# Feed-forward in column pairs: seven block products in place of eight on half of the k-tiles, weight block sums on VectorE

## The reference

```python
x = x + jnp.concatenate([ret, att], axis=-1) @ w_out[layer]
h = rms_norm(x, norm2_g[layer])
x = x + jnp.square(jax.nn.relu(h @ w_ff1[layer])) @ w_ff2[layer]
```

## Time and profile before

| | us |
|---|---|
| median of 3 runs | 1158.16 (1158.1 to 1158.98) |
| span of the profiled execution | 1156.3 |
| TensorE busy | 1149.4 (99%) |
| VectorE busy | 650.8 (56%) |
| ScalarE busy | 530.9 (46%) |

### The profile page before, as it was taken

One profiled execution on the slowest core, in us unless ns is written; L12 is line 12 of the kernel. 1 busy time (PEld: TensorE's weight loads), 2 busy tenths in 40 slices (PEclk: granted clock), 3 DMA queues, 4 the chain that ended last, 5 costly groups with the idle time before them and its releaser, 6 DMA issues.

```text
span 1156.3 us, 14920 instructions
## 1 busy us (share of the span) xinstructions
PE 1149.4 (99%) x5426; PEld 977.8 (85%) x5426; DVE 650.8 (56%) x845; ACT 530.9 (46%) x730; POOL 23.5 (2%) x26
## 2 busy tenths in 40 slices
PE   9999999999999999999999999999999999999998
PEld 8889889889888888888888888888888888888887
DVE  6667667667667555545545555554555555555543
ACT  6545445445444554444433445343444433444342
POOL 0000000000000000000000000000000000000000
PEclk9999999999999999999999999999999999999999
DMA  9745445445454545545555543555445555454552
GB/s 355 310 172 192 162 161 193 159 175 176 177 193 177 188 173 194 185 178 194 207 182 193 194 188 150 218 186 207 187 181 181 185 200 195 158 209 179 198 195 77
DMA packets 34918, 219.23 MB, mean 190 GB/s; under 512 B 3920, under 2 KB 4432, under 8 KB 12112
## 3 DMA queue, kind: packets, MB, share of 16 engines
q1 hardware_dynamic: 34896, 218.93, 52.3%
HBM read 216.81 MB, written 2.10 MB: 189 GB/s over the span
## 4 chain that ended last, share of the span: by engine, by line
PE 97%; DMA 2%; DVE 1%; SPq 0%; ACT 0%; issue 0%; ACTq 0%
PE acc L333 31%; PE acc L335 31%; PE acc L334 31%; DMA raw<-in_w_ret 1%; PE bankB L361 1%; PE bankA L361 1%; DMA raw<-in_w_att 1%; PE bankC L377 0%; PE bankC L388 0%; PE bankD L403 0%; PE bankD L383 0%; DVE w_lo L692 0%; PE bankA L395 0%; PE bankC L411 0%; PE bankC L412 0%
## 5 line engine op out<-in xcount | busy, mean ns | idle before, releaser
L692 DVE TENSOR_TENSOR w_lo<-raw,w_hi 128x1024 fp32r<-128x1024 f32 (+1 forms) x416 | 488.2, 1181 | 352.7 <-ACT w_hi L503 350.3
L503 ACT ACTIVATE w_hi<-raw 128x1024 fp32r<-128x1024 f32 (+1 forms) x416 | 420.9, 1025 | 354.2 <-PE acc L335 345.8
L333 PE MATMUL acc<-w_hi,hT_hi 128*128 128x512 f32 (+1 forms) x1024 | 392.1, 383 | 1.8 <-DVE w_lo L692 1.8
L335 PE MATMUL acc<-w_hi,hT_lo 128*128 128x512 f32 (+1 forms) x1024 | 385.1, 376 | 0.0
L334 PE MATMUL acc<-w_lo,hT_hi 128*128 128x512 f32 (+1 forms) x1024 | 384.7, 376 | 0.0
L333 PE MATMUL acc<-w_hi,zT_hi 128*128 128x512 f32 x640 | 250.2, 391 | 0.0
L335 PE MATMUL acc<-w_hi,zT_lo 128*128 128x512 f32 x640 | 249.2, 389 | 0.0
L334 PE MATMUL acc<-w_lo,zT_hi 128*128 128x512 f32 x640 | 249.0, 389 | 0.0
L333 PEld LDWEIGHTS acc<-w_hi,hT_hi 128*128 128x128 f32 x1024 | 192.4, 188 | 31.9 <-DVE w_lo L692 3.0
L335 PEld LDWEIGHTS acc<-w_hi,hT_lo 128*128 128x128 f32 x1024 | 192.2, 188 | 30.4
L334 PEld LDWEIGHTS acc<-w_lo,hT_hi 128*128 128x128 f32 x1024 | 192.5, 188 | 29.1
(11 more groups left out here) (109 smaller groups left out, 365.6 us busy)
## 6 DMA issues: line engine op xcount, KB each, us to landing
raw<-in_w_up SPq DMA_DIRECT2D x64, 1024.0 KB, 4.8
raw<-in_w_down SPq DMA_DIRECT2D x64, 1024.0 KB, 4.8
raw<-in_w_ret SPq DMA_DIRECT2D x32, 1024.0 KB, 4.8
raw<-in_w_att SPq DMA_DIRECT2D x28, 768.0 KB, 4.3
raw<-in_w_out SPq DMA_DIRECT2D x16, 1024.0 KB, 4.9
raw<-in_w_att SPq DMA_DIRECT2D x8, 384.0 KB, 7.0
xs<-in_x SPq DMA_DIRECT2D x4, 512.0 KB, 13.6
out<-xs SPq DMA_DIRECT2D x8, 256.0 KB, 4.3
```

The costliest lines, as they stand in the source:

```text
L333: nc.tensor.matmul(o, hi[:, k, tile_cols(m)], wh, start=first, stop=False)
L335: mm = nc.tensor.matmul(o, lo[:, k, tile_cols(m)], wh, start=False, stop=last)
L503: nc.scalar.activation(w_hi[:, q % SLOTS, 0:PIECE_KT * n], raw[:, q // 2, (q % 2) * PIECE_KT * n:(q % 2 + 1) * PIECE_KT * n], ACT.Copy).th ...
L692: nc.vector.tensor_tensor(w_lo[:, q % SLOTS, 0:PIECE_KT * n], raw[:, q // 2, (q % 2) * PIECE_KT * n:(q % 2 + 1) * PIECE_KT * n], w_hi[:, q ...
```

## The change

**Column pairs.** The feed-forward works in 16 pairs p of two column groups: of every four, two are up and two down. Of a pair's 16 k-tiles, the first 8 are a 2 x 2 block problem: two blocks of 4 k-tiles by two row tiles on the left, and two by two column groups on the right, where a block of the weights is one slab. These eight block products are made as seven of a Winograd scheme (`product`, 12 matmuls each): Q1, P5, P6, Q2, P7, P3, P4. The other 8 k-tiles are four slabs as before, R1 to R4 (`rest`, 24 matmuls each). R1 and R2 go to the first column group and R3 and R4 to the second.

**Steps of a body.** PE's body p makes the rest of pair p-1 between the products of pair p, in the order R1, Q1, R2, P5, R3, P6, R4, Q2, P7, P3, P4. The code is unrolled. `w_hi` and `w_lo` are rings of 3 slabs, and a conversion is one instruction of 128 x 2048 (`hi_slab`, `lo_slab`); `hi_slab(s)` waits until slab s-3 is used. `raw` has 5 slots.

**Sums of weights.** P5, P6, P7 and P4 need a sum of slabs in `raw`, made in place by VectorE (`sum_slabs`), ahead of the conversion.

**Sums of products.** Q1, P6 and P7 share a bank, so ScalarE copies Q1 to `q1` (`keep_q1`) before P6, and VectorE makes u1, u3, u2 and v4 (128 x 512 each) out of banks and these. Four outputs follow for a pair: for up pairs `up_sum` makes `hid`, and ScalarE has relu and square; for down pairs `add_products` and `add_bank` add twice to `xs`.

**Sums of activations.** The left operands are eleven forms of 128 x 512: seven for the products, four for the rest. The mixes (sums and differences) are VectorE's (`x_mix_of`, `d_mix_of`), hi parts ScalarE's (`x_hi_of`, `d_hi`), lo parts VectorE's (`x_lo_of`, `d_lo`). Those of the down pairs are spread over bodies p mod 4 = 1 and 2, those of x over the output projection and bodies 0 and 1. The last output projection group is the rest of body 0.

```diff
+            def product(p, step, hi, lo, form, bank, alone):
+
+                s = slab_no(p, step)
+                pe.wait_ge(slab_lo, s + 1)
+                wh, wl = w_hi[:, ring(s)], w_lo[:, ring(s)]
+                for t in range(SLAB_KT):
+                    cols = slice(t * N, (t + 1) * N)
+                    nc.tensor.matmul(bank[:], hi[:, form, tile_cols(t)], wh[:, cols], start=t == 0, stop=False)
+                    nc.tensor.matmul(bank[:], hi[:, form, tile_cols(t)], wl[:, cols], start=False, stop=False)
+                    mm = nc.tensor.matmul(bank[:], lo[:, form, tile_cols(t)], wh[:, cols], start=False,
+                                          stop=alone and t == SLAB_KT - 1)
+                mm.then_inc(slab_used, 1)
...
+                    forms(6)
+                    pe.wait_ge(q1_ok, p + 1)
+                    product(p, P6, hi, lo, S2N, bX, True)
+                if was_up:
+                    hid_blocks(prev, 0)
...
+            def sum_slabs(p, into, other, fresh):
+
+                r, q = PLAN[p, into][0], PLAN[p, other][0]
+                for name in fresh:
+                    dve.wait_ge(raw_in[PLAN[p, name][0]], PLAN[p, name][1])
+                nc.vector.tensor_tensor(raw[:, r, :], raw[:, r, :], raw[:, q, :], ALU.add).then_inc(summed, 1)
```

ScalarE in one body, for pairs with s = 11p, from `hi_slab(s + 2)` (R2) on:

```diff
+            def keep_q1(p):
+
+                act.wait_ge(slab_used, slab_no(p, Q1) + 1)
+                if p > 0:
+                    bank_read(act, p - 1, 0)
+                nc.scalar.activation(q1[:], bX[:], ACT.Copy).then_inc(q1_ok, 1)
...
+                hi_slab(s + 2)
+                if prev == 0:
+                    x_rest(OUT_GROUPS - 1)
+                if prev % 4 == 1 and prev >= 0:
+                    act.wait_ge(d_mix, 4 * (prev // 4) + 2)
+                    d_hi(S1, sd[:, 1, :])
+                    d_hi(A12, sd[:, 2, :])
+                    d_hi(A22, sd[:, 3, :])
+
+                hi_slab(s + 3)
...
+                hi_slab(s + 9)
+                if was_up:
+                    relu(prev, 0, 1)
+                    relu(prev, 1, 1)
+                    square(prev, 0, 1)
+                    square(prev, 1, 1)
+                if first_up:
+                    d_hi(A11, sd[:, 0, :])
+
+                hi_slab(s + 10)
```

VectorE in a body, its first steps and those around P6 to P3:

```diff
+                if p == 0:
+                    add_to_stream(G_LAST, 0, OUT_GROUPS - 2)
+                else:
+                    sum_u2(prev)
+                sum_slabs(p, "a", "b", ["b"])
+                lo_slab(s + 2)
...
+                lo_slab(s + 5)
+                if second_up:
+                    d_lo(g, 7, S4, sd[:, 2, :])
+                if kept == "U":
+                    up_sum(prev, 0, 0)
+                    up_sum(prev, 1, 0)
+                if kept == "D":
+                    add_bank(prev, 0, 0)
+                    add_bank(prev, 1, 0)
+
+                sum_slabs(p, "b", "d", [])
+                lo_slab(s + 6)
+
+                lo_slab(s + 7)
+
+                sum_slabs(p, "a", "e", ["e"])
...
+                sum_u1(p)
+                lo_slab(s + 8)
+                if kept == "U":
+                    up_sum(prev, 0, 1)
+                else:
+                    add_bank(prev, 0, 1)
+
+                lo_slab(s + 9)
```

More of the change, by code:

```diff
@@ L219, in piece_cols, with piece, kind, weights @@
             return PIECE_KT * n
+        def piece(buffer, q, first, last):
+            start = q % SLOTS * PIECE_KT * N
+            return buffer[:, start + first:start + last]
         def tile_cols(m):
             return slice(m * P, (m + 1) * P)
+        def kind(p):
+            return "R" if p < 0 else "UUDD"[p % 4]
+        def weights(p):
+            if p < 0:
+                return w_out, OUT_GROUPS - 2
+            g, c = p // 4, 2 * (p % 2)
+            return (w_up, 4 * g + c) if kind(p) == "U" else (w_down, 4 * g + c)
@@ new lines, in slab_no, with raw_of, ring, bank_read @@
+        def slab_no(p, step):
+            return STEPS * p + step if p < PAIRS else STEPS * PAIRS + (R1, R2, R3, R4).index(step)
+        def raw_of(s):
+            p, step = step_of(s)
+            name = READ_AT[step]
+            return PLAN[p - 1 if name[0] == "R" else p, name]
+        def ring(s):
+            return slice((s + 2) % RING * SLAB_KT * N, ((s + 2) % RING + 1) * SLAB_KT * N)
+        def bank_read(engine, p, n):
+            if kind(p) == "U":
+                engine.wait_ge(up_ok, 8 * (p // 4) + 4 * (p % 4) + n + 1)
+            elif kind(p) == "D":
+                engine.wait_ge(acc_read_dve, added(p) + n + 1)
+            else:
+                engine.wait_ge(acc_read_dve, 2 * (OUT_GROUPS - 2) + n + 1)
@@ L224, in hybrid_block, with added @@
+        def added(p):
+            return 2 * OUT_GROUPS + 4 * (2 * (p // 4) + p % 4 - 2)
         block = ctx.enter_context(nc.Block())
@@ L427, in _ @@
             in_order = list(range(KT))
-            EVEN = [False]
             pe.wait_ge(ident_ok, 1)
@@ new lines, in rest @@
+            def rest(p, step, hi, lo, form, banks, opens, closes):
+                s = slab_no(p, step)
+                pe.wait_ge(slab_lo, s + 1)
+                wh, wl = w_hi[:, ring(s)], w_lo[:, ring(s)]
+                for m in range(MT):
+                    for t in range(SLAB_KT):
+                        cols = slice(t * N, (t + 1) * N)
+                        nc.tensor.matmul(banks[m][:], hi[:, form + m, tile_cols(t)], wh[:, cols],
+                                         start=opens[m] and t == 0, stop=False)
+                        nc.tensor.matmul(banks[m][:], hi[:, form + m, tile_cols(t)], wl[:, cols], start=False, stop=False)
+                        mm = nc.tensor.matmul(banks[m][:], lo[:, form + m, tile_cols(t)], wh[:, cols], start=False,
+                                              stop=closes and t == SLAB_KT - 1)
+                    if closes and m == 0:
+                        mm.then_inc(half_used, 1)
+                mm.then_inc(slab_used, 1)
@@ new lines, in rest_out @@
+            def rest_out(step, j):
+                s = slab_no(0, step)
+                pe.wait_ge(slab_lo, s + 1)
+                wh, wl = w_hi[:, ring(s)], w_lo[:, ring(s)]
+                for m in range(MT):
+                    if j == 0:
+                        pe.wait_ge(acc_read_dve, 2 * (OUT_GROUPS - 3) + m + 1)
+                    bank = (bZ, bW)[m]
+                    for t in range(SLAB_KT):
+                        k = MIX_ORDER[SLAB_KT * j + t]
+                        cols = slice(t * N, (t + 1) * N)
+                        nc.tensor.matmul(bank[:], zT_hi[:, k, tile_cols(m)], wh[:, cols], start=j == 0 and t == 0, stop=False)
+                        nc.tensor.matmul(bank[:], zT_hi[:, k, tile_cols(m)], wl[:, cols], start=False, stop=False)
+                        mm = nc.tensor.matmul(bank[:], zT_lo[:, k, tile_cols(m)], wh[:, cols], start=False,
+                                              stop=j == SLABS - 1 and t == SLAB_KT - 1)
+                    if j == SLABS - 1 and m == 0:
+                        mm.then_inc(half_used, 1)
+                mm.then_inc(slab_used, 1)
```

691 lines of the change are left out of this document (498 added, 193 removed).

## The result

The changed kernel takes **1185.6 us** (1184.0 to 1186.2, four runs) beside 1158.3 of the kernel before: 1.0234 times as long, with a 95% interval of 1.022 to 1.0249. The profiled execution has a span of 1183.9, against 1156.3. The prediction was 1182, with "slower" as its side.

The account below looks back on a forecast made before the run. TensorE, without waits, was taken to bound the kernel. From a span of 1156.3 us, 43.5 won and 67.8 lost gave 1180.6; the runs' median lies 1.9 above the profiled span, so 1182 us, range 1163 to 1203.

Parts of the forecast that it names:

- What it removes: On TensorE, a column pair needs 180 products instead of 192; sixteen pairs save 43.5 us.
- VectorE's slab at 2.21, ScalarE's at 1.87: Queue time in us of one 128x2048 slab conversion on each engine, extrapolated from smaller sizes.
- Down bodies, 40.95 and 41.5: Bodies p mod 4 = 3 or 0 just fit: 40.95 us, or 41.5 behind a second up body.
- First up body, +2.5: Body p mod 4 = 1: P4's conversion queues behind relus, squares and a split; 45.1 us over a floor of 42.6.
- Second up body, +11.7: Body p mod 4 = 2: ScalarE and VectorE take turns waiting, delaying P5, R3, P6 and P4; 54.3 us over 42.6.
- Entry, +1.9: Last projection group but one: forms of x and two squares precede ScalarE's next piece; about 10.0 us against 8.2.
- body 0, +0.9: First feed-forward body: R4 comes late behind the x splits, 0.9 us over the floor of 42.6.
- Body 1, +1.7: Second feed-forward body: its rest forms come late, adding 1.7 us.
- Rival B: VectorE's slab costs 2.27 us; down bodies have no slack, up to 14 us more, 1190 to 1200; chance 0.12.
- D: Weight slabs land late by DMA; at 250 GB/s 2.2 us in each of 15 bodies, 1215 us; chance 0.06.
- C: The two-slab lead swallows TensorE's waits, making the kernel faster, at best 1115 us; chance 0.14.
- Rival E, the clock: TensorE's clock may halve after the wait before R3: up to 5.4 us each, 22 in all, 1204 us; chance 0.06.
- rival A: Waits stand in the queues as walked through each kind of body: 1168 to 1196 us; chance 0.62.

Follow-up runs that it names:

- run 6: Changed kernel with the reorders of run 1 and Run 2 together, and without the 64 weight sums on VectorE: 1117.65 us.
- run 1: Changed kernel with P4's conversion moved ahead, in both up bodies, of relus, squares and a split on ScalarE and of splits on VectorE: 1164.56 us.
- run 5: Changed kernel with unread filler matmuls on TensorE, 15 ahead of R3 in second up bodies and 10 ahead of P4 in both up bodies: 1181.38 us.
- Run 2: Changed kernel with VectorE's mixes mostly earlier and splits later in the second up body, and TensorE waiting for fewer forms before P6 and Q2: 1158.46 us.
- Run 9: Kernel of run 3 with ScalarE's squares at the entry and in body 0 moved later: 1133.4 us.
- run 3: Changed kernel with the reorders of run 1 and Run 2 together, same instructions on every engine: 1135.86 us.
- run 7: Kernel of run 3 with one of the four weight sums (b + d) made by GpSimd in all pairs but the first: 1167.95 us.
- run 8: Kernel of run 3 with the weight sum b + d made by GpSimd in the second up bodies alone: 1137.75 us.
- run 4: Changed kernel in its own order, without the 64 weight sums on VectorE and ScalarE's wait for them: 1164.23 us.

## Why the prediction was right, point by point

- **What it removes**: 192 x 0.2267 = 43.5 us. Right: all bodies of run 6 are at 42.8 and 40.8, the floors it gave.
- **VectorE's slab at 2.21, ScalarE's at 1.87.** A slot here is the time from an instruction's start to its successor's. The slots measure 2.20 (641.34 to 643.54 in the down body before the round shown: a lo part, then the next operation) and 1.9 (the record is 1.91, its successor starts 1.8 to 1.9 later). Of the bounds, the lower was it. VectorE's round was put at 165.6 and is 166.26; ScalarE's at 99.4 and is 102.22. That a sum costs what a subtraction does was right (2283 and 2286 ns here), but the two rows that it was read from (684 and 683 at 512) are both additions, and show no subtraction.
- **Down bodies, 40.95 and 41.5.** 41.06 and 41.06 to 41.4: "just fits" was right, with VectorE busy 41.39 of 41.39. Of the bodies behind a second up body, 3 and 7 take 41.3 and 41.4; 11 and 15, which the slow P4 ahead made start late, take 41.1 like the rest.
- **First up body, +2.5.** P4 was to start at 42.26 and starts at 42.61; the body takes 45.4 (45.1 and a share of the restart gaps). The reason given, P4's hi part behind relus, squares and a split, is what run 1 took away, and the wait went. Bodies 9 and 13 are 1.6 over that, body 1 some 1.4 for the same reason: the clock.
- **Second up body, +11.7.** P5 at 14.86, R3 at 21.45, P6 at 29.3 were predicted; body 6 has 14.80, 21.44, 29.28. It takes 54.7 for 54.3, the difference being restart gaps, which the sum had apart. In the other three the steps up to P6 come some 1.5 earlier than predicted, and the slow clock in P4, which the sum didn't have, puts it on again at the end. Their 54.7 is thus the predicted length by another way, though not by chance: the queues of the other two engines keep their times, and only the start of the body moves (R3 of body 10 starts 66.84 behind the start of body 9, and 66.83 in run 5). Run 2 shows the cause of the waits: with splits and mixes moved, R3 is there at 16.8.
- **P6's releaser, q1.** In the changed kernel TensorE's wait before P6 is 0.51 with "issue" as its releaser, which alone would not show it. ScalarE's q1 copy is at 723.40, behind the output (L1308), and P6 starts at 724.10; and in run 5, where R3 ends earlier, ScalarE's q copy is named as the releaser of four waits, up to 2.2 us. As predicted.
- **Entry, +1.9, body 0, +0.9.** Body 0 starts 1.98 late and takes 43.52 for 42.6. Run 9 gives back 2.5 of these 2.9.
- **Body 1, +1.7.** Measured against the other first up bodies at the slower clock, 0.9; against body 5, 2.5. It started R2 at 9.24 for 8.16, 1.1 late; so the rest forms cost 1.1 there, not 1.7, and the other 1.4 is the clock (seven slow matmuls from 509.78).
- **Rival B** (a slab at 2.27): it is 2.20. **D** (slabs land late): in all of the changed kernel ScalarE's 180 hi parts wait six times for a weight DMA, 10.9 us in sum and never over 1.9, and the down bodies, which would have shown it, are at 41.1. **C** (the waits swallowed): no.
- **Rival E, the clock.** It does fall, after R3's wait as the rival said, and after P4's, as it didn't. But it was put at up to 5.4 for each R3, all of the 24 matmuls at half speed; six to eight are slow, up to 1.6 us, and those at R3 hide behind q1. Run 5 prices it at 4.2 us, by medians, in place of 22. So rival A held, with a small part of E in it, which the sum had at nothing: 1.4 to 1.6 in each of bodies 1, 9 and 13 is more than the 3.3 by which the span (1183.9 for 1180.6) is over the sum. The sum was as near as that because small terms were put too high by as much: body 1's rest forms by 0.6, and bodies 11 and 15 by 0.4 each.
- **What the prediction didn't say**: that VectorE's load decides mainly in the second up body. It weighed VectorE by the round (165.6 of 166.9) and found that it fits; by the body it is 45.0 of 42.6 in one kind and 39.4 in another. Here that did not matter, since the queues cost more; with the order repaired it is most of what is left (run 3).

## What to carry over

When work moves to an engine that stays below 100%, do not stop at its total: walk the queues of both engines that hand work to each other, in order, through each kind of body, and look for an instruction that waits (a split of a mix) ahead of one that others wait for (a slab's conversion). Here the order, and not the load, was 50 of the 71 us lost (runs 3 and 6), and reordering without removing an instruction turned 2.3% slower into 2.2% faster (run 9). And compare loads by the stage in which buffers couple the engines, not by the round.

## What the runs showed of the hardware

- A sum of 128x2048 in SBUF had a record of 6.6 to 10.0 us on GpSimd and of 2.28 on VectorE. In all 19 cases (runs 7 and 8) GpSimd ended 4.5 us after the last VectorE instruction on two SBUF tiles that had gone ahead of it, some of which had begun after it; the next such instruction of VectorE stood still until it ended (5.74 for 2.29). What decides which of the two goes first, the rows don't show. An idle GpSimd is no free place for such work.
- In the changed kernel TensorE ran six to eight matmuls at 1.2 GHz after waits of 3.3 to 3.7 us. After waits of 2.6 it did so in six cases and not at all in two. The slow matmuls began anywhere from the restart itself (874.55) to 1.6 us behind it (509.78, restart at 508.20). The other runs bear this out: in run 1, six to twelve slow matmuls behind each of its four waits of 3.6; behind waits of 1.9 to 2.7, six to eight in 22 of 35 cases (runs 2, 4, 5, 7 and the changed kernel); behind waits of up to 1.7, none. What told the cases apart, the rows don't show.
- Slower matmuls on the waiting engine can make the next wait vanish: the engine behind gets ahead by as much. The clock's price was 4.2 us, where ten stretches of up to 1.6 would be some 15 if all of them counted.
